# Reordering the opening of a two-layer kernel: a side product, the transposes of x and the modulation's columns

## The reference, cut to what matters

```
mod  = silu(c) @ w_ada + b_ada                 # 6 vectors of 1024: shift1, scale1, gate1, ...
h    = rms_norm(x, norm1_g) * (1 + scale1) + shift1      # first layer, input of everything
proj = h @ w_in                                # its first pieces used: the values (va, vb)
...
x    = x + gate * (p_2 @ w_ple_2)              # the very end of the second layer
```

## Time and profile before

| | |
|---|---|
| median of three runs | 1991.64 us (1990.22 to 1991.87) |
| profiled execution | 1991.4 us |
| its span, first to last instruction | 1989.6 us |
| mean granted TensorE clock | 0.998 |
| TensorE (PE) busy | 1958.7 us, 98% |
| VectorE (DVE) busy | 1066.0 us, 54% |
| ScalarE (ACT) busy | 806.9 us, 41% |
| DMA, mean | 100 GB/s |

### The profile page before, as it was taken

The page is one execution under the profiler, slowest core; times in us unless marked ns, Lnnn a source line. Parts: engine busy times, 40 slices in busy tenths (PEclk is TensorE's granted clock), DMA queues, the critical chain, the costliest instruction groups (busy, mean ns, idle before and its releaser), DMA issues.

```text
span 1989.6 us, 24259 instructions
## 1 busy us (share of the span) xinstructions
PE 1958.7 (98%) x9224; PEld 1602.7 (81%) x9224; DVE 1066.0 (54%) x1695; ACT 806.9 (41%) x1355; POOL 118.0 (6%) x138
## 2 busy tenths in 40 slices
PE   7999999999999999999999999999999999999998
PEld 6778777888888888888888888878888888888887
DVE  6687877455433543475545454466653453434354
ACT  5343555534322223343232323487752342322343
POOL 2140000002000000200000000000000200000010
PEclk9999999999999999999999999999999999999999
DMA  9842212122333433322222222211223332323321
GB/s 365 328 170 85 64 58 92 64 85 77 98 95 89 112 84 87 108 80 85 86 84 84 84 84 74 65 56 45 65 89 103 129 104 86 105 90 100 98 92 64
DMA packets 196578, 199.64 MB, mean 100 GB/s; under 512 B 7547, under 2 KB 170448, under 8 KB 194064
## 3 DMA queue, kind: packets, MB, share of 16 engines
q1 hardware_dynamic: 192416, 175.15, 28.3%
q0 software_dynamic: 4080, 23.40, 3.0%
HBM read 194.33 MB, written 4.19 MB: 100 GB/s over the span
## 4 chain that ended last, share of the span: by engine, by line
PE 91%; DVE 3%; ACT 3%; issue 1%; POOL 1%; DMA 1%; SPq 0%; POOLq 0%; DVEq 0%; ACTq 0%
PE bank L774 47%; PE bank L1281 4%; PE bank L1027 4%; PE bank L739 4%; PE bank L864 4%; PE bank L850 3%; PE bank L1541 3%; PE bank L1353 2%; PE bank L1082 2%; PE bank L1011 1%; PE bank L894 1%; PE bank L977 1%; PE bank L1301 1%; PE bank L1217 1%; PE bank L1129 1%
## 5 line engine op out<-in xcount | busy, mean ns | idle before, releaser
L1657 ACT ACTIVATE w_hi<-raw 128x2048 fp32r<-128x2048 f32 (+4 forms) x165 | 285.1, 1729 | 405.3 <-PE bank L774 296.3
L2410 DVE TENSOR_TENSOR w_lo<-raw,w_hi 128x2048 fp32r<-128x2048 f32 (+4 forms) x163 | 336.7, 2066 | 147.4 <-ACT w_hi L1657 145.5
L774 PE MATMUL bank<-h_hi,w_hi 128*128 128x512 f32 x864 | 337.6, 391 | 0.0
L774 PE MATMUL bank<-h_hi,w_lo 128*128 128x512 f32 x864 | 336.3, 389 | 0.0
L774 PE MATMUL bank<-h_lo,w_hi 128*128 128x512 f32 x864 | 336.2, 389 | 0.0
L774 PEld LDWEIGHTS bank<-h_hi,w_lo 128*128 128x128 f32 x864 | 162.2, 188 | 34.2
L774 PEld LDWEIGHTS bank<-h_lo,w_hi 128*128 128x128 f32 x864 | 162.2, 188 | 34.1 <-issue 0.5
L774 PEld LDWEIGHTS bank<-h_hi,w_hi 128*128 128x128 f32 x864 | 162.2, 188 | 33.9 <-issue 0.5
L774 PE MATMUL bank<-u_hi,w_hi 128*128 128x512 f32 x256 | 100.9, 394 | 0.0
L774 PE MATMUL bank<-u_hi,w_lo 128*128 128x512 f32 x256 | 100.4, 392 | 0.0
L774 PE MATMUL bank<-u_lo,w_hi 128*128 128x512 f32 x256 | 99.4, 388 | 0.0
(11 more groups left out here) (580 smaller groups left out, 4148.2 us busy)
## 6 DMA issues: line engine op xcount, KB each, us to landing
raw<-in_w_in SPq DMA_DIRECT2D x49, 1024.0 KB
raw<-in_w_ff SPq DMA_DIRECT2D x44, 512.0 KB
raw<-in_w_up SPq DMA_DIRECT2D x16, 1024.0 KB
raw<-in_w_down SPq DMA_DIRECT2D x16, 1024.0 KB
raw<-in_w_o SPq DMA_DIRECT2D x8, 1024.0 KB
raw<-in_w_br SPq DMA_DIRECT2D x8, 1024.0 KB
raw<-in_w_in SPq DMA_DIRECT2D x13, 512.0 KB
raw<-in_w_ff SPq DMA_DIRECT2D x8, 768.0 KB
```

What stands on the lines that cost most here:

```text
L774: last = nc.tensor.matmul(dst, a, b, start=k == n == 0, stop=k == last_k and n == 2)
L1657: nc.scalar.activation(w_hi[:, slot, 0:width], raw[:, slot, 0:width], ACT.Copy).then_inc(hi_done, 1)
L2410: v.tensor_tensor(w_lo[:, slot, 0:width], raw[:, slot, 0:width], w_hi[:, slot, 0:width].bitcast(F32), ALU.subtract).then_inc(lo_done, 1)
```

## The change: one order of the opening for another

TensorE now makes both halves of the side product back to back (banks 4 to 7, then 0 to 3), then six tiles of x in the banks that ScalarE has emptied (`X_BANK`), then the transpose of the small vectors and `columns(0)`. ScalarE copies banks 4 to 7 out ahead of making the diagonals, then banks 0 to 3 (all four; DVE's copy of bank 3 is gone), then six tiles of x. POOL's two stores wait for the same copies as before, which come at other places now. Nothing changes in SP's program.

```diff
+        X_BANK = (4, 5, 6, 7, 0, 1, 6, 4)
 ...
                 pool.wait_ge(sem("p_copied"), 4)
                 nc.gpsimd.dma_start(ple_kept[:, 0:4, :], xT[:, 4:8, :]).then_inc(sem("ple_saved"), 16)
-                pool.wait_ge(sem("p_copied"), 7)
-                pool.wait_ge(sem("p_made"), 3)
+                pool.wait_ge(sem("p_copied"), 8)
                 nc.gpsimd.dma_start(ple_kept[:, 4:8, :], ple_b[:]).then_inc(sem("ple_saved"), 16)
 ...
             def turn_x(f):
-                at = f if f < 7 else 4
-                if f == 7:
-                    pe.wait_ge(sem("xT_ready"), 5)
+                at = X_BANK[f]
+                if f < 6:
+                    pe.wait_ge(sem("p_copied"), f + 1)
+                elif f == 6:
+                    pe.wait_ge(sem("xT_ready"), 3)
+                else:
+                    pe.wait_ge(sem("small_exp"), 3)
 ...
                 ple_half(0)
-                for f in range(4):
+                ple_half(1)
+                for f in range(6):
                     turn_x(f)
-                ple_half(1)
-                pe.wait_ge(sem("p_copied"), 4)
+                pe.wait_ge(sem("xT_ready"), 1)
                 pe.wait_ge(sem("vectors_in"), 16 * 16)
                 pe.wait_ge(sem("head_vectors_in"), 16 * 6)
                 nc.tensor.transpose(bank[4][:, 0:NVR], vrows[0:NVR, :], ident[0:NVR, 0:NVR]).then_inc(sem("small_mm"), 1)
+                pe.wait_ge(sem("xT_ready"), 4)
                 columns(0)
-                pe.wait_ge(sem("small_exp"), 3)
-                turn_x(4)
-                turn_x(5)
 ...
             def values():
-                pe.wait_ge(sem("p_copied"), 7)
-                pe.wait_ge(sem("p_made"), 3)
+                pe.wait_ge(sem("p_copied"), 8)
+                pe.wait_ge(sem("xT_ready"), 6)
 ...
             def ple_half(half):
-                    if half:
-                        pe.wait_ge(sem("xT_ready"), n + 1)
 ...
             (ScalarE, after the square root)
+                act.wait_ge(mm_done, U0["ple_in"] + 1)
+                for n in range(4):
+                    nc.scalar.activation(xT[:, 4 + n, :], bank[4 + n][:], ACT.Copy).then_inc(sem("p_copied"), 1)
                 act.wait_ge(sem("small_sums"), 2)
                 for t in range(QT):
                     nc.scalar.activation(diag[t], ident[:], ACT.Copy, scale=small[:, t:t + 1]
 ...
-                for f in range(4):
+                for n in range(4):
+                    if n < 3:
+                        act.wait_ge(sem("p_mm"), n + 3)
+                    else:
+                        act.wait_ge(mm_done, U0["ple_in"] + 2)
+                    nc.scalar.activation(ple_b[:, n, :], bank[n][:], ACT.Copy).then_inc(sem("p_copied"), 1)
+                for f in range(6):
                     x_out(f)
-                for n in range(4):
-                    act.wait_ge(mm_done, U0["ple_in"] + 1)
-                    nc.scalar.activation(xT[:, 4 + n, :], bank[4 + n][:], ACT.Copy).then_inc(sem("p_copied"), 1)
-                for n in range(3):
-                    act.wait_ge(sem("p_mm"), n + 3)
-                    nc.scalar.activation(ple_b[:, n, :], bank[n][:], ACT.Copy).then_inc(sem("p_copied"), 1)
                 act.wait_ge(sem("small_mm"), 2)
                 nc.scalar.activation(vT[:], bank[4][:, 0:NVR], ACT.Copy).then_inc(sem("small_exp"), 1)
                 split(2)
                 high1(0)
-                for f in range(4, KD):
+                for f in range(6, KD):
 ...
             (VectorE, ahead of make_h1(0))
-                dve.wait_ge(mm_done, U0["ple_in"] + 2)
-                v.tensor_copy(ple_b[:, 3, :], bank[3][:]).then_inc(sem("p_made"), 1)
```

More of the change, by code:

```diff
@@ L1726, in x_out @@
                     act.wait_ge(sem("x_mm"), f + 1)
-                    nc.scalar.activation(xnT[:, f, :], bank[f if f < 7 else 4][:], ACT.Copy).then_inc(sem("xT_ready"), 1)
-                for f in range(4):
-                    x_out(f)
-                for n in range(4):
-                    act.wait_ge(mm_done, U0["ple_in"] + 1)
-                    nc.scalar.activation(xT[:, 4 + n, :], bank[4 + n][:], ACT.Copy).then_inc(sem("p_copied"), 1)
-                for n in range(3):
-                    act.wait_ge(sem("p_mm"), n + 3)
-                    nc.scalar.activation(ple_b[:, n, :], bank[n][:], ACT.Copy).then_inc(sem("p_copied"), 1)
+                    nc.scalar.activation(xnT[:, f, :], bank[X_BANK[f]][:], ACT.Copy).then_inc(sem("xT_ready"), 1)
+                for n in range(4):
[5 more added lines that the diff above has]
+                for f in range(6):
+                    x_out(f)
                 act.wait_ge(sem("small_mm"), 2)
```

## The result

The changed kernel takes 1995.95 us (median of 13 runs, 1994.53 to 1996.95), the kernel before in the same sessions 1991.65 us (1990.09 to 1993.23): 4.3 us more, a ratio of 1.0023 with a 95% interval of 1.0015 to 1.003. The profiled execution of the changed kernel took 1996.95 us, the longest of the 13, so its rows show more loss than the median; its span is 5.6 us longer than the span before.

What follows compares the result with a forecast made beforehand. TensorE, busy 98% of the span, was taken as the bound, losing time only where it stands or runs at low clock. Late `split(2)` 2.05 plus low clock 1.65 made 3.7, on 1991.4: 1995.1 us, range 1991.8 to 1997.2.

Steps and rivals of the forecast that it cites:

- the forecast's own edge: Upper limit of the main forecast's band, 1992.9 to 1995.6 us, which was given a chance of 0.52.
- clearly slower: Rival: unit 2 lands at 33.8 and the low clock outlasts 3.3 us; up to 1997.4 us, chance 0.33.
- TensorE and ScalarE recomputed: Opening: columns at 28.2, 2.6 us earlier; `split(2)` could start at 28.9; the change so far gains 2.25 us.
- The stores cross the queue: POOL's two stores, issued near 21.1 and 24.5, take the DMA engines and hold q1's loads up by 4.8 us.
- When unit 2 lands: Load read by `split(2)`: held from 27.8 to 33.2, so `split(2)` starts at 33.25, 2.05 us later than before.
- The upper end: Latest landing given for unit 2 behind the stores: 27.8 + 6.0 = 33.8 us.
- the ladder of landings: Earlier trace's loads after 25.1: they would end at 41.3, but the last landed at 47.3, 6.0 us late.
- the middle: Unit 2's landing taken as 33.2 us, between a lower end of 32.6 and an upper of 33.8.
- The clock: First value product: after a 7.5 us TensorE stop the clock falls to 0.50, costing 1.65 us (bounds 0 and 3.3).
- The sum: Late `split(2)` 2.05 plus low clock 1.65 give 3.7 us, which nothing downstream takes up: 1995.1 us.
- It gains: Rival: the stores' packets start only after unit 2 lands, `split(2)` at 28.9; 1990.8 or 1989.2 us, chance 0.09.
- Half of it: Rival: only the first store is ahead of unit 2's end, `split(2)` −0.9, clock +1.65; 1992.1 us, chance 0.06.

Runs made afterwards that it cites:

- e1: Changed kernel with POOL's two stores held until ScalarE has split weight unit 2: 1991.89 us, ratio 1.0004 to the kernel before.
- e6: Changed kernel with both stores held until unit 2 is split and two of six tiles of x moved behind the columns: 1989.19 us, ratio 0.9991.
- e7: Changed kernel with both stores held until unit 2 is split, and 12 unused matmuls behind the columns: 1989.93 us, ratio 0.9992.
- e3: Kernel before, old order, with two same-size stores of x tiles issued as early as in the changed kernel: 1995.68 us, ratio 1.0025.
- e2: Changed kernel with only the second store held until ScalarE has split unit 2, the first going early: 1993.49 us, ratio 1.0012.
- e5: Changed kernel with each early store cut in four by feature tile, for smaller packets and the same bytes: 1993.99 us, ratio 1.0013.
- e4: Changed kernel with 30 unused matmuls behind the columns to keep TensorE busy, stores still early: 1993.87 us, ratio 1.0014.
- e8: Kernel before with 11 filler matmuls in TensorE's 2.56 us stop before the tiles of x: 1990.28 us, ratio 0.9996.

## Why the prediction was right

1995.1 us was forecast, with a range of 1991.8 to 1997.2; 1995.95 was measured, 0.35 us past the forecast's own edge of 1995.6. The mechanism was right in each step; both sizes were too small, and the time lies where the rival "clearly slower" put it. By its steps:

- **TensorE and ScalarE recomputed: right.** Columns at 28.2, measured 28.25. `split(2)` free to start at 28.9, measured 29.1 as the end of what precedes it. The 2.25 us that the new order would gain alone showed as a first value product 1.8 us earlier in e1, 2.2 in e6 and 2.4 in e7.
- **The stores cross the queue: right, and the decisive step.** Issued at 21.4 and 24.5 (21.1 and 24.5 forecast). e3 has the loss without the new order, e1 the new order without the late load, e2 a part for one store. The hold-up was priced in bytes; e5 shows that the size of the packets sets it. The price came out near all the same, since it was read from the same stores, with the same packets, in the earlier trace rows.
- **When unit 2 lands: right in kind, 0.7 short.** 33.25 was forecast, 33.94 measured. The upper end, 33.8, from the ladder of landings, was the right one; the middle was taken. That this execution's first loads came later (VectorE's first chunk at 17.42, not 17.12) does not explain it: in e4 that chunk starts at 17.08, and `split(2)` still at 33.87. The 2.05 us of the sum are 2.2 by e4's median.
- **The clock: right in kind, too small.** 1.65 was taken, from a stretch of 3.3 us; the low clock lasted through at least 5.6 us of work in the profiled execution (2.90 lost), and cost 2.1 us in the medians.
- **The sum: 3.7 forecast, 4.3 measured.** Nothing downstream took it up, as said: the second splits start 5.51 us later (67.93 and 62.42) in the profiled executions, as much as the two parts add up to.
- **The rivals.** "It gains" needed the stores to wait for VectorE; they were at work from 25.2 on, 3.8 us after the first issue, though VectorE was in `ada` then; the lag was 3.95 before, with VectorE past `ada`. "Half of it" is what e2 built on purpose. "Clearly slower" fits the medians by its own terms: the landing reached its upper end, the low clock lasted longer than 3.3 us, and together they come to 4.3 us, where the rival asked for more than 4.2. It was given 0.33, against 0.52 for the forecast. That the changed kernel is slower is clear of noise (the interval of the ratio begins at 1.0015); that it is so by more than 0.2% is not shown, since the interval holds both sides of 1.002.

The experiments add what the forecast only argued: with the stores out of the way and TensorE at work behind the columns, the new order is worth 1.7 us (e7) or, with two tiles moved, 2.5 us (e6) in the medians. Most of this is again the clock: the old order meets the low clock at 20 us, and filling that stop alone gave it 1.4 us (e8). Against e8 the order of e6 wins 1.1 us (1990.28 − 1989.19).

## What to carry to other kernels

When a step is moved ahead, list the DMAs that hang on it and look at what is then in flight: a store that costs nothing late can push out the load that the next stage waits for. Where DMA engines are saturated, the size of its packets decides how much it takes: with 4 KB instead of 8 KB the load came 2.9 us sooner (e5). And count the stop that a shorter chain opens on TensorE: keep some real matmul work for it, or the clock takes back what the reordering won.

## What the runs showed of the hardware that was not expected

- Behind the columns the clock fell sooner than the stops of the kernel before let expect. In the changed kernel it was 1.00 in 28.30 to 30.10 and 0.50 from 30.70, within 0.6 us of the columns' end, though TensorE had worked without a stop from 14 us on. In the kernel before, a stop of 1.6 us left it at 1.00, and in the stop of 2.56 us it was still 1.00 until work resumed near 20 us. With work right behind the columns (e4, e6, e7) it stayed at 1.00. Why it fell so early is left open.
- The stop at 62 us did not always leave the clock alone. In e1's profiled execution it fell near 65.9 us, 1.1 us after work had resumed:

```profile
62.00:65.00 3.00, 1.24 (x6) 0.74 (x5) 2.93 (x6) 3.00 (x4) 0.00 (x0) 1.00 1.00 423
65.90:69.30 3.40, 3.40 (x10) 2.65 (x9) 3.40 (x3) 0.63 (x1) 0.00 (x0) 0.50 0.08 10
```

- A longer stop did not always cost more. At 1.00 the 16 matmuls of the first value product take about 3.9 us. They took 6.19 us behind a stop of 3.05 us (e1) and 5.73 us behind one of 4.50 us (e2); behind 3.00 us (e3) it was 5.50, behind 4.98 us (e5) 6.70 and behind 8.00 us (the changed kernel) 6.78. These are single profiled executions. What decides how long the low clock lasts after work resumes is left open.
